# Expert weights by quarters of a head, w_query loaded once, and eight places for gathered rows instead of sixteen

## The chip, the cores and the metric

The kernel runs on one core of one Trainium2 chip, in float32. The metric is device time in microseconds, the median of several executions.

## The reference, cut to what matters

One layer of an encoder over 512 tokens of 1024 numbers: adaLN, a mixing sub-layer (8 heads of neighbourhood attention, 4 of differential attention, one output projection `w_out`), a LayerNorm, and then PEER retrieval, in which each token picks 16 of 16384 experts in each of 8 heads. The change is about PEER and what leads into it:

```python
qc = (xc @ w_query).reshape(PEER_CHUNK, PEER_HEADS, 2, PEER_DKEY // 2)
s_half = jnp.einsum('chpk,pnk->chpn', qc, sub_keys, preferred_element_type=jnp.float32)
top_s, top_i = lax.top_k(s_half, PEER_TOPK)
cand_s = (top_s[:, :, 0, :, None] + top_s[:, :, 1, None, :]).reshape(PEER_CHUNK, PEER_HEADS, -1)
cand_i = (top_i[:, :, 0, :, None] * PEER_NKEYS + top_i[:, :, 1, None, :]).reshape(PEER_CHUNK, PEER_HEADS, -1)
best_s, best_j = lax.top_k(cand_s, PEER_TOPK)
expert = jnp.take_along_axis(cand_i, best_j, axis=-1)
g = jax.nn.softmax(best_s, axis=-1)
u_e = expert_down[expert]
act = jax.nn.gelu(jnp.einsum('chkd,cd->chk', u_e, xc), approximate=False)
v_e = expert_up[expert]
return jnp.einsum('chk,chkd->cd', (g * act).astype(xc.dtype), v_e)
```

`w_query` is 1024 x 2048, `expert_down` and `expert_up` are 16384 x 1024. After PEER, `x = LN(alpha*x + (1+gate)*f)`, scaled by `ln2_g` and shifted by `ln2_b`.

## The kernel before, in words

Tokens lie in four tiles of 128, one token on each partition. A first phase (`FIRST_GROUPS`, made by `phase_a_groups`) does the modulation, the input projection, and attention as 48 items of a tile and a head (`ATT`). A group is a piece of PE work that ends in one PSUM bank and is evacuated by DVE (kinds in `ON_DVE`) or ACT. `FIRST_TILE` sets groups of tile 0's mixing output and its PEER query between the attention items: mix_t and out at items 17 and 18, the transposed u at 28, four query groups at 30 to 33, key scores at 34. `LN_FIRST` and `CHOOSE_FIRST` do the same for DVE: tile 0's LayerNorm at items 19 to 25, the choice of experts of head 0 at items 36 to 43.

A "head" from here on is one of 32 pairs of a tile and a PEER head, in the order of `HEAD_AT` (tile 0 heads 0 to 3, tile 1 heads 0 to 3, tile 0 heads 4 to 7, and so on). `choose(head, step)` (L1078) does top-k on DVE in 16 steps: it writes 16 expert numbers per token to `expert_idx`.

The second phase is a stream of 1024 gathers, 512 "down" and 512 "up" (16 a head). Each is one indirect DMA from POOL (L594) that fetches one expert row of 4 KB for each of 128 tokens, 0.524 MB, into a place. `gather_order` (L190) sets their order: down `at`, then up `at - UP_LAG`, with `UP_LAG` 19. POOL waits in `wait_for_place` (L572) until the place's last use is over. The first 280 gathers go round eight places (`FIRST_PLACES`); then eight more are added, in the slots of `w_out` (`OUT_SLOT`), which POOL does after a wait for out(3,1) (L591).

Who uses what:
- DVE runs the loop at L1323. For each down it makes the dot product with the token's u (L1334), which frees the place. In the first eight dots of a head it also chooses the next head, two steps a dot. `weigh` (L1285) stands after the third dot of the next head (`WEIGH_AT`) and makes that head's 16 weights at once. `LN_AT` and `ADD_AT` set tiles' LayerNorms and mixing adds after given dots, `RESIDUAL_AFTER` the residual (L1296) and, a head later, `finish` (L1313) of a tile.
- ACT waits for 16 dots and runs one gelu per head (`expert_gelu`, L852), the next head's exponentials (`gate`, L844), and 16 `diagonals` (L974): each is the identity scaled by one weight. It also evacuates PE's groups, `EVAC_AFTER` 3 diagonals behind the step in which the group ended, and takes the square roots (`ln_deviation`, `deviation`).
- PE runs the loop at L801. For each up it multiplies the diagonal by the gathered row, in two halves of 512 (L810; each is two matmuls in the profile), into the tile's sum. Behind it, it does the parts that `SCHEDULE` (L133) gives to that step: transposes, query parts (L642), out parts (L668), key scores (L676). An entry is (first step, parts per step, groups); a query or out group has eight parts.
- SP loads weights. `w_query` comes in four chunks of 2.10 MB, and `QUERY_SLOT` has only two slots for them: chunks 0 and 1 before the stream and again in it, chunks 2 and 3 twice in it, eight loads (L486, L500, L509 to L517).

Of the kernel before, what the change touches and what calls it, by code (L numbers as in the profile page):

```python
# [19 lines left out]
ALU = mybir.AluOpType  # L20
# [50 lines left out]
QUERY_SLOT = [1, 0, 1, 0]  # L71
FIRST_PLACES, PLACES = 8, 16
UP_LAG = TOPK + 3
WEIGH_AT = 2
# [16 lines left out]
def octet_runs(t):  # L91
# [5 lines left out]
FIRST_TILE = {17: [("mix_t", (0, 0)), ("mix_t", (0, 1)), ("out", (0, 0))], 18: [("out", (0, 1))],  # L97
              28: [("u_first", (0,)), ("u_first", (1,))],
              30: [("query", (0, 0, 0, 1))], 31: [("query", (0, 1, 0, 1))], 32: [("query", (0, 2, 0, 1))],
              33: [("query", (0, 3, 0, 1))], 34: [("key_scores", (0, 0))]}  # L100
LN_FIRST = {19: (0,), 20: (1,), 21: (2,), 22: (3,), 23: (4,), 24: (5,), 25: (6, 7)}
CHOOSE_FIRST = {36 + i: (2 * i, 2 * i + 1) for i in range(8)}


def phase_a_groups():
# [9 lines left out]
    for a in range(len(ATT) + 3):  # L115
# [4 lines left out]
        if a >= 3:  # L120
            g += [("values", (a - 3,))]
        g += FIRST_TILE.get(a, [])
    g += [("mix_t", (1, s)) for s in range(2)] + [("out", (1, s)) for s in range(2)]
# [9 lines left out]
SCHEDULE = [(0, 4, [("u_t", (1, s)) for s in range(2)]),  # L133
            (4, 3, [("query", (0, b, 1, 1)) for b in range(4)]), (19, 1, [("key_scores", (0, 1))]),
            (20, 3, [("query", (1, b, 1, 1)) for b in range(4)]), (35, 1, [("key_scores", (1, 1))]),
            (36, 2, [("query", (2, b, 0, 2)) for b in range(4)]),
            (55, 1, [("key_scores", (2, 0))]), (58, 1, [("key_scores", (2, 1))]),
            (59, 1, [("mix_t", (2, s)) for s in range(2)]), (64, 1, [("out", (2, s)) for s in range(2)]),
            (80, 2, [("query", (3, b, 0, 2)) for b in range(4)]), (99, 1, [("key_scores", (3, t)) for t in range(2)]),
            (101, 1, [("mix_t", (3, s)) for s in range(2)]), (106, 1, [("out", (3, s)) for s in range(2)]),  # L140
            (144, 1, [("u_t", (t, s)) for t in (2, 3) for s in range(2)]),
            (150, 1, [("query", (0, b, 2, 2)) for b in range(4)]), (185, 1, [("key_scores", (0, t)) for t in (2, 3)]),
            (190, 1, [("query", (1, b, 2, 2)) for b in range(4)]), (223, 1, [("key_scores", (1, t)) for t in (2, 3)]),
            (230, 1, [("query", (2, b, 2, 2)) for b in range(4)]),
            (264, 1, [("key_scores", (2, 2))]), (312, 1, [("key_scores", (2, 3))]),
            (316, 1, [("query", (3, b, 2, 2)) for b in range(4)]), (349, 1, [("key_scores", (3, t)) for t in (2, 3)])]
# [43 lines left out]
def gather_order():  # L190

    order = []
    for at in range(SETS + UP_LAG):
        order += [("down", at)] if at < SETS else []
        order += [("up", at - UP_LAG)] if at >= UP_LAG else []
    return order
# [40 lines left out]
def build(nc, x, c, w_ada, b_ada, w_in, w_out, na_rpb, t5_bias, lambda_q1, lambda_k1, lambda_q2,  # L237
# [3 lines left out]
    with ctx:  # L241
# [55 lines left out]
        for slot in (T5_SLOT,) + tuple(OUT_SLOT):  # L297
            places += [w_flat[slot][:, i * D:(i + 1) * D] for i in range(4)]
# [1124 lines left out]
```

## Time and profile before

| | us |
|---|---|
| median of 3 runs | 1805.6 |
| their range | 1800.57 to 1809.73 |
| the profiled execution | 1808.22 |
| its span | 1806.1 |
| PE busy | 1487.8 (82%) |
| DVE busy | 1137.8 (63%) |
| POOL busy | 1004.0 (56%) |
| ACT busy | 386.9 (21%) |

The span runs from the first to the last instruction; the execution's own time is 2.1 us more. Shares are of the span. DMA moved 612.29 MB in it, of which 536.94 MB on the gathers' queue, a mean of 339 GB/s; 607.97 MB were read from HBM. The mean granted TensorE clock was 0.968.

### The profile page before, as it was taken

The numbers are of one execution on the slowest core, as the hardware profiler recorded it, in microseconds if no ns is written. First come the engines' busy times: TensorE is split into PE (matmuls) and PEld (weight loads), VectorE is DVE, ScalarE is ACT, GpSimd is POOL, SyncE is SP. The second block draws the span as 40 slices with busy tenths as digits, with TensorE's granted clock in tenths as the row PEclk, the third lists the DMA queues.
The fourth block names the chain that finished last, engine by engine and source line by source line (L and its number), as shares of the span: only waits on it lengthen the run. The fifth ranks groups of instructions, "written<-read, shape, count | busy, mean of one in ns | idle before, by whom it ended". The sixth has DMA issues, their size and how long they took to land.

```text
span 1806.1 us, 14345 instructions
## 1 busy us (share of the span) xinstructions
PE 1487.8 (82%) x4112; PEld 689.3 (38%) x4112; DVE 1137.8 (63%) x2715; ACT 386.9 (21%) x983; POOL 1004.0 (56%) x1057
## 2 busy tenths in 40 slices
PE   5899988974889898887988979877799777777776
PEld 4444455642445344332433434322343222222222
DVE  5453056679567576878666766677666666666741
ACT  1111143422122212312112221221212111111220
POOL 2100000034667676677776767777777777777770
PEclk9799999896999999999999999999999999999998
DMA  9677320166999999999999999999999999999992
GB/s 311 240 261 212 116 70 12 13 230 211 405 406 409 394 409 407 362 409 410 409 408 408 409 408 409 409 409 410 409 409 409 409 409 409 409 408 410 406 410 94
DMA packets 194307, 612.29 MB, mean 339 GB/s; under 512 B 31263, under 2 KB 31671, under 8 KB 194071
## 3 DMA queue, kind: packets, MB, share of 16 engines
q0 software_dynamic: 147456, 536.94, 75.2%
q1 hardware_dynamic: 46423, 73.21, 12.1%
q10 hardware_dynamic: 352, 1.25, 0.2%
q8 instruction: 34, 0.56, 0.1%
q14 instruction: 42, 0.34, 0.1%
HBM read 607.97 MB, written 3.34 MB: 338 GB/s over the span
## 4 chain that ended last, share of the span: by engine, by line
DMA 40%; PE 26%; POOL 15%; DVE 8%; issue 7%; ACT 1%; SPq 1%; DVEq 0%; POOLq 0%
DMA big<-in_expert_up,expert_idx 14%; DMA region_v<-in_expert_up,expert_idx 13%; PE pair L604 11%; POOL big L594 10%; PE pair L810 10%; DMA big<-in_expert_down,expert_idx 8%; POOL region_v L594 4%; DMA region_v<-in_expert_down,expert_idx 4%; PE pair L642 2%; DVE big L1334 2%; DMA big<-in_w_ada 1%; PE pair L668 1%; DVE region_v L1334 1%; ACT big L907 1%; DVE big L1242 1%
## 5 line engine op out<-in xcount | busy, mean ns | idle before, releaser
L810 PE MATMUL pair<-big 128*128 128x512 f32 x1416 | 690.8, 612 | 181.4 <-DMA big<-in_expert_up,expert_idx 139.4
L1334 DVE CUSTOM_DVE_ANT_0 big<-big,pair 128x1024 f32<-128x1024 f32 x346 | 421.8, 1220 | 273.9 <-DMA big<-in_expert_down,expert_idx 272.5
L810 PEld LDWEIGHTS pair<-big 128*128 128x128 f32 x1416 | 244.7, 190 | 554.5 <-issue 485.1
L594 POOL DMA_INDIRECT big<-in_expert_up,expert_idx x354 | 336.4, 950 | 142.4 <-PE pair L810 83.8
L594 POOL DMA_INDIRECT big<-in_expert_down,expert_idx x346 | 330.6, 956 | 122.9 <-issue 99.4
L810 PE MATMUL pair<-region_v,big 128*128 128x512 f32 x632 | 308.6, 612 | 64.5 <-DMA region_v<-in_expert_up,expert_idx 63.3
L1334 DVE CUSTOM_DVE_ANT_0 region_v<-region_v,pair 128x1024 f32<-128x1024 f32 x166 | 202.5, 1220 | 130.9 <-DMA region_v<-in_expert_down,expert_idx 129.2
L604 PE MATMUL pair<-big 128*128 128x512 f32 (+1 forms) x496 | 203.9, 605 | 1.9 <-DVE big L1210 1.9
L594 POOL DMA_INDIRECT region_v<-in_expert_down,expert_idx x166 | 161.9, 975 | 69.6 <-issue 45.1
L981 ACT ACTIVATE big<-ident,big 128x128 f32<-128x128 f32 x512 | 158.5, 389 | 187.8 <-DVE big L1293 185.9
L810 PEld LDWEIGHTS pair<-region_v,big 128*128 128x128 f32 x632 | 110.7, 190 | 223.7 <-issue 214.4
L560 POOL TENSOR_SCALAR small<-small 128x4 f32<-128x4 f32 (+1 forms) x7 | 1.6, 233 | 348.2 <-DVE small L1266 289.9
L594 POOL DMA_INDIRECT region_v<-in_expert_up,expert_idx x158 | 149.9, 949 | 67.2 <-PE pair L810 35.4
L642 PE MATMUL pair<-big 128*128 128x256 f32 (+1 forms) x640 | 144.3, 342 | 6.9 <-DVE big L1058 6.1
L642 PEld LDWEIGHTS pair<-big 128*128 128x128 f32 x640 | 107.3, 195 | 96.1 <-issue 87.1
L604 PEld LDWEIGHTS pair<-big 128*128 128x128 f32 (+1 forms) x496 | 88.2, 198 | 100.3 <-issue 96.5
L890 ACT ACTIVATE big<-pair 128x512 f32<-128x512 f32 (+2 forms) x74 | 33.3, 456 | 415.8 <-PE pair L642 262.0
L855 ACT ACTIVATE big<-big 128x16 f32<-128x16 f32 x32 | 6.9, 216 | 456.1 <-DVE big L1334 456.0
L1179 DVE SCALAR_TENSOR_TENSOR big<-big,small 128x512 f32<-128x512 f32 x78 | 62.2, 798 | 2.8
L958 ACT ACTIVATE big<-pair 128x512 f32<-128x512 f32 (+3 forms) x70 | 37.6, 541 | 120.0 <-PE pair L604 99.7
L668 PE MATMUL pair<-big 128*128 128x512 f32 x128 | 60.8, 594 | 1.6 <-ACT big L890 1.6
L907 ACT ACTIVATE big<-big,small 128x256 f32<-128x256 f32 (+1 forms) x64 | 39.0, 610 | 73.8 <-DVE small L1242 73.8
(145 smaller groups left out, 1008.0 us busy)
## 6 DMA issues: line engine op xcount, KB each, us to landing
big<-in_w_ada SPq DMA_DIRECT2D x12, 2048.0 KB, 15.6
big<-in_w_query SPq DMA_DIRECT2D x8, 2048.0 KB, 19.1
big<-in_w_in SPq DMA_DIRECT2D x6, 2048.0 KB, 15.9
big<-in_expert_up,expert_idx POOLq DMA_INDIRECT x354, 17.7
big<-in_expert_down,expert_idx POOLq DMA_INDIRECT x346, 17.7
big<-in_w_out SPq DMA_DIRECT2D x2, 2048.0 KB, 10.3
big<-na_scr SPq DMA_DIRECT2D x24, 128.0 KB, 4.0
region_v<-in_expert_down,expert_idx POOLq DMA_INDIRECT x166, 12.9
```

Of the source, the lines that this page charges most:

```text
L594: nc.gpsimd.indirect_dma_start(places[place], None, (expert_down if kind == "down" else expert_up)[0], bass.IndirectOffsetOnAxis(expert_id ...
L604: last = nc.tensor.matmul(ps, a, b, start=(i == 0), stop=(i == len(pairs) - 1))
L642: return nc.tensor.matmul(ps[:, 0:n * P], w_slot[QUERY_SLOT[c]][:, k, b * P:(b + 1) * P], src, start=(k == 0), stop=(k == KB - 1))
L668: return nc.tensor.matmul(ps[:, :], src, w_slot[OUT_SLOT[s]][:, k, :], start=(k == 0), stop=(k == KB - 1))
L810: last = nc.tensor.matmul(pair[t % 2][:, s * HALF:(s + 1) * HALF], diag[:, j, :], places[place][:, s * HALF:(s + 1) * HALF], start=(h == 0 ...
L890: nc.scalar.activation(dst, ps, ACT.Copy).then_inc(act_evac, 1)
L907: nc.scalar.activation(exps, raw, ACT.Exp, bias=row_min[:, slot:slot + 1], scale=-1.0, accum_out=row_sum[:, slot:slot + 1]).then_inc(exp_d ...
L958: nc.scalar.activation(dst, ps, ACT.Copy, scale=scale).then_inc(act_evac, 1)
L981: nc.scalar.activation(diag[:, j, :], ident[:, :], ACT.Copy, scale=weights[:, head % 2, j:j + 1]).then_inc(diag_done, 1)
L1179: last = v.scalar_tensor_tensor(out=acc, in0=w[:, k, :], scalar=c_exp[:, k:k + 1], in1=acc, op0=ALU.mult, op1=ALU.add)
L1242: v.tensor_tensor_reduce(out=dst, in0=scored, in1=bias, scale=1.0, scalar=3.0e38, op0=ALU.add, op1=ALU.min, accum_out=row_min[:, slot:slot ...
L1334: v.tensor_tensor_reduce(out=places[place], in0=places[place], in1=u_cur[:, :], scale=1.0, scalar=0.0, op0=ALU.mult, op1=ALU.add, accum_ou ...
```

## The change

Nothing else of the result changes; these parts of the order and of the storage do:
- `QUERY_SLOT` gives each chunk of `w_query` a slot of its own; chunks 2 and 3 take the slots of `w_out` once out(3,0) and out(3,1) are done. There are four loads instead of eight.
- Eight places throughout, with no wait for out(3,1) on POOL.
- gelu, weighing and diagonals go by quarters of a head (four dots). The ups follow their downs by 7 instead of 19; the first up comes after down 14, then two ups for each down until they have caught up.
- Tile 0's LayerNorm, query and key scores stand one to five items earlier in attention; heads 0 and 1 are both chosen there (items 32 to 47). out(1,1) moves from ahead of PE's loop into its first steps; the other groups of `SCHEDULE` move, and so do LayerNorms, adds and residuals.
- In the LayerNorms of the second phase and tile 0's, (x - mean) * rstd * gain + shift is two operations on DVE instead of three.

```diff
-QUERY_SLOT = [1, 0, 1, 0]
-FIRST_PLACES, PLACES = 8, 16
-UP_LAG = TOPK + 3
-WEIGH_AT = 2
+QUERY_SLOT = [1, 0] + OUT_SLOT
+PLACES = 8
+QUARTER = 4
+UP_LAG = QUARTER + 3
+FIRST_UP = 14
...
+FIRST_TILE = {16: [("mix_t", (0, 0)), ("mix_t", (0, 1)), ("out", (0, 0))], 17: [("out", (0, 1))],
+              25: [("u_first", (0,)), ("u_first", (1,))],
+              26: [("query", (0, 0, 0, 1))], 27: [("query", (0, 1, 0, 1))], 28: [("query", (0, 2, 0, 1))],
+              29: [("query", (0, 3, 0, 1))], 30: [("key_scores", (0, 0))]}
+LN_FIRST = {18: (0,), 19: (1,), 20: (2, 3, 4), 21: (5,), 22: (6, 7)}
+CHOOSE_FIRST = {32 + i: (i // 8, 2 * (i % 8)) for i in range(16)}
...
+SCHEDULE = [(0, 1, [("out", (1, 1))]), (14, 1, [("mix_t", (2, s)) for s in range(2)]),
+            (22, 4, [("u_t", (1, s)) for s in range(2)]),
+            (24, 4, [("query", (0, b, 1, 1)) for b in range(4)]), (34, 1, [("key_scores", (0, 1))]),
+            (35, 4, [("query", (1, b, 1, 1)) for b in range(4)]), (45, 1, [("key_scores", (1, 1))]),
+            (46, 2, [("out", (2, s)) for s in range(2)]),
+            (56, 1, [("mix_t", (3, 0))]), (59, 1, [("mix_t", (3, 1))]), (62, 1, [("out", (3, s)) for s in range(2)]),
+            (80, 2, [("query", (2, b, 0, 2)) for b in range(4)]), (98, 1, [("key_scores", (2, t)) for t in range(2)]),
+            (100, 1, [("query", (3, b, 0, 2)) for b in range(4)]), (133, 1, [("key_scores", (3, t)) for t in range(2)]),
...
+LN_FROM = {1: 21, 2: 88, 3: 168}
+ADD_AT = {8: (1, 0), 20: (1, 1), 60: (2, 0), 65: (2, 1), 81: (3, 0), 89: (3, 1)}
+RESIDUAL_AFTER = {12: 0, 16: 1, 28: 2}
+WEIGHED = [max(QUARTER * (n + 1), 13) for n in range(HEADS * QUARTER - 1)]
...
+    for at in range(SETS):
+        order.append(("down", at))
+        for _ in range(2):
+            if at >= FIRST_UP and ups <= at - UP_LAG:
+                order.append(("up", ups))
+                ups += 1
+    order += [("up", at) for at in range(ups, SETS)]
...
-            load_query(2, ("query", (0, 3, 1, 1)))
-            load_query(3, ("query", (1, 3, 1, 1)))
-            load_query(0, ("query", (2, 3, 0, 2)))
-            load_query(1, ("query", (3, 3, 0, 2)))
+            load_query(2, ("out", (TILES - 1, 0)))
+            load_query(3, ("out", (TILES - 1, 1)))
...
-            load_query(2, ("query", (0, 3, 2, 2)))
-            load_query(3, ("query", (1, 3, 2, 2)))
...
-            def expert_gelu(head):
-                act.wait_ge(dot_done, (head + 1) * TOPK)
-                nc.scalar.activation(acts[:, head % 2, :], at_head(dots, head), ACT.Gelu).then_inc(gelu_done, 1)
+            def expert_gelu(head, q):
+                lo = q * QUARTER
+                act.wait_ge(dot_done, head * TOPK + lo + QUARTER)
+                nc.scalar.activation(acts[:, head % 2, lo:lo + QUARTER], at_head(dots, head)[:, lo:lo + QUARTER],
+                                     ACT.Gelu).then_inc(gelu_done, 1)
...
             for head in range(HEADS):
+                for q in range(QUARTER):
+                    if head * QUARTER + q in deviation_before:
+                        ln_deviation(deviation_before[head * QUARTER + q])
+                    expert_gelu(head, q)
+                    diagonals(head, q)
+                    if q == 2 and head + 1 < HEADS:
+                        gate(head + 1)
...
+            def weigh(head, q):
+                k, lo = head % 2, q * QUARTER
+                if q == 0:
+                    dve.wait_ge(gate_done, head + 1)
+                    link(v.reciprocal(gate_sum[:, k:k + 1], gate_sum[:, k:k + 1]))
+                    if head >= 2:
+                        dve.wait_ge(diag_done, (head - 1) * TOPK)
+                dve.wait_ge(gelu_done, head * QUARTER + q + 1)
+                v.scalar_tensor_tensor(out=weights[:, k, lo:lo + QUARTER], in0=gate_exps[:, k, lo:lo + QUARTER],
+                                       scalar=gate_sum[:, k:k + 1], in1=acts[:, k, lo:lo + QUARTER],
+                                       op0=ALU.mult, op1=ALU.mult).then_inc(weight_done, 1)
```

## Rows read from the trace of the kernel before

**Rows 1.** The page: DMA's busy tenths and GB/s in 40 slices.
```profile
DMA  9677320166999999999999999999999999999992
GB/s 311 240 261 212 116 70 12 13 230 211 405 406 409 394 409 407 362 409 410 409 408 408 409 408 409 409 409 410 409 409 409 409 409 409 409 408 410 406 410 94
```

**Rows 2.** The page: the chain that ended last, by engine.
```profile
DMA 40%; PE 26%; POOL 15%; DVE 8%; issue 7%; ACT 1%; SPq 1%; DVEq 0%; POOLq 0%
```

**Rows 3.** Windows: us, busy (count) by engine, PEclk, DMA share, GB/s.
```profile
384.50:450.00 65.50, 34.65 (x136) 21.45 (x135) 59.05 (x140) 12.05 (x29) 34.56 (x34) 0.77 0.77 259
450.00:600.00 150.00, 130.56 (x426) 70.15 (x424) 90.10 (x217) 30.03 (x82) 101.28 (x108) 0.98 1.03 405
600.00:625.00 25.00, 21.41 (x54) 9.91 (x55) 15.84 (x44) 11.42 (x27) 15.26 (x17) 0.86 1.01 383
625.00:725.00 100.00, 92.67 (x260) 47.02 (x258) 68.42 (x162) 15.79 (x42) 71.47 (x75) 1.00 1.03 409
725.00:750.00 25.00, 20.09 (x46) 8.00 (x47) 19.50 (x36) 7.52 (x16) 15.35 (x16) 1.00 0.88 324
800.00:1750.00 950.00, 768.80 (x1777) 303.24 (x1776) 651.90 (x1538) 192.14 (x500) 692.73 (x728) 1.00 1.03 409
```

**Rows 4.** DMA issues (450:600, 1200:1500, page): count, KB, us to landing.
```profile
region_v<-in_expert_down,expert_idx POOLq DMA_INDIRECT x28, 7.9
...
big<-in_expert_up,expert_idx POOLq DMA_INDIRECT x86, 18.1
...
big<-in_w_query SPq DMA_DIRECT2D x8, 2048.0 KB, 19.1
```

**Rows 5.** Groups of instructions by form: busy, mean ns, idle before.
```profile
L981 ACT ACTIVATE big<-ident,big 128x128 f32<-128x128 f32 x512 | 158.5, 389 | 187.8 <-DVE big L1293 185.9 <-PE pair L810 1.9
...
L855 ACT ACT_TABLE_LOAD x32 | 41.1, 1283 | 0.6
...
L1293 DVE SCALAR_TENSOR_TENSOR big<-big 128x16 f32<-128x16 f32 x32 | 7.5, 235 | 1.1
...
L855 ACT ACTIVATE big<-big 128x16 f32<-128x16 f32 x32 | 6.9, 216 | 456.1 <-DVE big L1334 456.0
```

**Rows 6.** Timeline, start of the stream: start, us, engine, line.
```profile
384.46 1.22 POOL L594 DMA_INDIRECT region_v<-in_expert_down,expert_idx  x1 [0.20 <-issue]
...
389.16 1.22 DVE L1334 CUSTOM_DVE_ANT_0 region_v<-region_v,pair 128x1024 f32<-128x1024 f32 x1 [2.13 <-DMA region_v<-in_expert_down,expert_idx]
...
407.32 0.68 DVE L1058 TENSOR_TENSOR big<-pair,mods 128x512 f32<-128x512 f32 x1
...
438.83 3.75 PE L810 MATMUL pair<-big 128*128 128x512 f32 x4 [23.47 <-ACT big L981]
```

**Rows 7.** Timeline of PE: three query parts; an up, an out part.
```profile
466.41 0.83 PE L642 MATMUL pair<-big 128*128 128x128 f32 x6
...
628.80 1.88 PE L810 MATMUL pair<-region_v,big 128*128 128x512 f32 x4
630.52 1.02 PE L668 MATMUL pair<-big 128*128 128x512 f32 x2
```

**Rows 8.** Timeline at the dip: DVE waits for ACT.
```profile
731.63 0.16 DVE L1039 RECIPROCAL small<-small 128x1 f32<-128x1 f32 x1 [4.01 <-ACT small L842]
```

**Rows 9.** Windows of attention, tiles 2 and 3, by the first scores of each.
```profile
303.80:343.40 39.60, 34.59 (x225) 28.11 (x224) 23.96 (x79) 17.83 (x52) 2.08 (x4) 0.91 0.20 27
343.40:379.60 36.20, 28.81 (x143) 18.91 (x142) 29.74 (x115) 17.06 (x51) 1.28 (x2) 0.86 0.04 18
```

**Rows 10.** The tail: timeline, a piece of the chain, a window.
```profile
1755.32 1.22 DVE L1334 CUSTOM_DVE_ANT_0 big<-big,pair 128x1024 f32<-128x1024 f32 x1 [1.32 <-DMA big<-in_expert_down,expert_idx]
...
1756.71 34.59 PE pair L810 x80
...
1795.99 0.81 DVE L1317 TENSOR_SCALAR big<-big,small 128x1024 f32<-128x1024 f32 x1
...
1770.00:1781.00 11.00, 11.00 (x27) 4.93 (x26) 0.00 (x0) 0.00 (x0) 0.00 (x0) 1.00 0.07 29
```

More of the change, by code:

```diff
@@ L122, in phase_a_groups @@
         g += FIRST_TILE.get(a, [])
-    g += [("mix_t", (1, s)) for s in range(2)] + [("out", (1, s)) for s in range(2)]
+    g += [("mix_t", (1, s)) for s in range(2)] + [("out", (1, 0))]
     g += [("u_t", (0, s)) for s in range(2)]
@@ L132 @@
 FIRST_GROUPS = phase_a_groups()
[L133 to L146, printed above, removed]
@@ L190, in gather_order @@
 def gather_order():
[L192 to L195, printed above, removed]
+    order, ups = [], 0
+    for at in range(SETS):
[5 more added lines that the diff above has]
+    order += [("up", at) for at in range(ups, SETS)]
     return order
 GATHERS = gather_order()
-FIRST_GATHERS = 280
 PLACE_OF, LAST_USE, USES = {}, {}, {}
@@ L296, in build @@
         places = [region_v[:, i, :] for i in range(4)]
-        for slot in (T5_SLOT,) + tuple(OUT_SLOT):
-            places += [w_flat[slot][:, i * D:(i + 1) * D] for i in range(4)]
+        places += [w_flat[T5_SLOT][:, i * D:(i + 1) * D] for i in range(4)]
         na_place_sb = mods[0:T5_BUCKETS, 0:2, :].rearrange("p t (e m) -> p (t e) m", m=2 * P)
@@ L628, in query_weights @@
             def query_weights(c, first, n):
-                loads = {(0, 0): 1, (0, 1): 1, (1, 0): 1, (1, 1): 1, (2, 0): 2, (3, 0): 2, (0, 2): 3, (1, 2): 3,
-                         (2, 2): 4, (3, 2): 4}[c, first]
+                loads = 1 if c < 2 else 2
                 slot = QUERY_SLOT[c]
@@ L893, in _ @@
                 ps = bank_of(g)
+                if (kind, args) == ("mix_t", (1, 1)):
+                    gate(0)
                 if kind in ("u_first", "mix_t", "u_t", "query", "key_scores"):
@@ L972, in _, with diagonals @@
                       .then_inc(t5_written, 16)
-            def diagonals(head):
-                act.wait_ge(weight_done, head + 1)
-                for j in range(TOPK):
+            def diagonals(head, q):
+                act.wait_ge(weight_done, head * QUARTER + q + 1)
+                for j in range(q * QUARTER, (q + 1) * QUARTER):
                     at = head * TOPK + j
@@ L1280, in _ @@
                         ln_step(0, step)
[L1281 to L1294 removed]
+                    if args[0] in CHOOSE_FIRST:
+                        head, step = CHOOSE_FIRST[args[0]]
+                        choose(head, step)
+                        choose(head, step + 1)
+            def weigh(head, q):
[9 more added lines that the diff above has]
+                                       op0=ALU.mult, op1=ALU.mult).then_inc(weight_done, 1)
             def residual(t):
@@ L1336, in _ @@
                                            accum_out=dots[:, at:at + 1]).then_inc(dot_done, 1)
-                    if j == WEIGH_AT and head > 0:
-                        weigh(head - 1)
-                    if j < TOPK // 2 and head + 1 < HEADS:
+                    for n in range(WEIGHED.count(at)):
+                        first = WEIGHED.index(at) + n
+                        weigh(first // QUARTER, first % QUARTER)
+                    if 0 < head < HEADS - 1 and j < TOPK // 2:
                         choose(head + 1, 2 * j)
                         choose(head + 1, 2 * j + 1)
-                    for group in ADD_AT.get(at, ()):
-                        add_mix(*group)
-                    if j >= TOPK // 2 and head in LN_AT:
-                        ln_step(LN_AT[head], j - TOPK // 2)
+                    if at in ADD_AT:
+                        add_mix(*ADD_AT[at])
+                    for row_tile, first in LN_FROM.items():
+                        if 0 <= at - first < 8:
+                            ln_step(row_tile, at - first)
                 if head in RESIDUAL_AFTER:
```

74 lines of the change are left out of this document (25 added, 49 removed).

## The prediction

> **What bounds the kernel now.** I read the page's slices first. From slice 20 of 40 on, DMA stands at 9 tenths and some 409 GB/s in every slice but the last [rows 1]. The chain that ended last says the same: 40% is DMA, 15% POOL, which issues the gathers, 26% PE [rows 2]. In 950 us late in the stream PE is busy 769 and DVE 652 [rows 3]. So from about 385 us on the kernel is a stream of 1024 gathers of 0.524 MB, and at 409 GB/s each costs 1.28 us, a down and an up together 2.56. The windows then show where the stream is not full: 259 GB/s in the first 65.5 us, 383 and 324 GB/s in two stretches of 25 us, 405 between [rows 3]. Against 409 that is 24.0, 1.6, 5.2 and 1.5 us, 32 us lost. Behind the stream, from 1781 to 1806, is a tail of 25 us in which PE, and then DVE, work alone. Ahead of it attention is bound by the chain PE, DVE, ACT, not by DMA.
>
> **Loads of w_query: eight become four.** Each moves 2.10 MB [rows 4]; two of the four that stay are loaded before the stream or at its start, as now. Four fewer run beside a full DMA: 4 x 2.10 MB / 409 GB/s = 20.5 us off the path, -20.5. The median of 19.1 us to landing is shared time and not the price. The first kept load (chunk 2) is issued after step 69 and needed at step 80: 11 x 2.56 = 28 us against those 19 us, covered by 9 us; if that cover went, PE would wait. The load of chunk 3 has over 20 steps. SP then goes to the ln2 rows at the 176th dot, needed at the 208th, 82 us later.
> The Trainium skill, DMA: Bandwidth & Descriptors, section Specifications, gives a core about 358 GB/s from HBM; by it the four loads would be worth an estimated 23.4 us. The trace moves 409 GB/s for 950 us on end, so the measurement decides.
>
> **Eight places instead of sixteen.** Up to the 280th gather the kernel already runs on eight: issue to landing is then 7.9 us, later 18.1 [rows 4], and between 625 and 725 us eight places gave the same 409 GB/s as sixteen do [rows 3]. In steady state I cost this at nothing. What shrinks is tolerance. A gather issued into an idle DMA is used 4.7 us after its issue [rows 6], 3.4 without its own 1.28. A place comes round after 8 x 1.28 = 10.3 us, so a consumer must be done 10.3 - 1.28 - 3.4 = 5.6 us after landing: DVE (1.22 for a dot) may be 4.4 us late, PE (1.9 for an up) 3.7. Later than that, DMA idles one for one.
> The Trainium skill, same page, Anatomy of one DMA - SWDGE (gpsimd) path, gives 2.0 us plus the bytes for a transfer, an estimated 3.2 us where the row shows 4.7. By it each stall below would be 1.5 us shorter, the sum some 6 us lower; the row decides.
>
> **Work by quarters.** There are 96 more gelus (0.22 us, ACT) and 96 more weighings (0.23 us, DVE) [rows 5]. Table loads stay at two a head, since gate comes once a head between two gelus. DVE is busy 652 of 950 us [rows 3], so idle for 31% of a quarter's 10.3 us, 3.2 us, and holds a weighing of 0.23 us with a link of the same order. A quarter's gelu is issued at its last dot and needed one dot later, 2.56 us; ACT's quarter is 0.22 + 4 x 0.39 us. Where ACT evacuates a PE group it waits for that step's up, which lands seven downs behind; most groups end one step before a multiple of four, which leaves two downs of room. Cost 0 in steady state.
>
> **The start of the stream.** Now head 1 is chosen between its first eight dots: from the first dot (389.16) to the mixing add (407.32) are 18.2 us, 8 dots take 9.2, so one choice is 9.0 us of DVE. Adds and LayerNorm of tile 1 follow, and the first up stands at 438.83 [rows 6]. After the change downs 0 to 13 need only their dots (1.2 against 1.28 us), and up 0 lands near 408. Ups then come two for each down, one per 1.92 us, while PE does the eight parts of out(1,1): 1.72 (628.80 to 630.52) + 0.86 for an out part's two matmuls, 2.57 us a step [rows 7]. It falls 5 us behind and up to 9 with the wait for its start: about 4 us beyond the tolerance. The three weighings after dot 13 pass through ACT's diagonals in turn, about 3.5 us of DVE: 2 lost. PE starts after idling; the first up at 438.83, after 23 us idle, took 3.75 us instead of 1.9: 3 us. With the fill of 3.4 us that makes 12.4 instead of 24.0. Bounds: 3.4 and 24.
> Later, the parts of queries 0 and 1 of tile 1 go four to a step: three took 0.83 us [rows 7], four make 1.72 + 1.11 = 2.83, in eight steps 2.2 us late, within tolerance. out(2,.) goes two parts a step: 1.72 + 1.72 = 3.43 us, eight times 0.87 = 7 us late; 3.3 beyond, with a rest from before it 4.5 lost. The dip at 732 is DVE waiting 4 us for ACT's deviation, behind ACT's evacuations [rows 8]; LayerNorm 2 (dots 88 to 95) still meets query groups, LayerNorm 3 no longer does. With three residuals (4 us of DVE each) I take 4 us, bounds 0 and 12. Together 8.5 where the trace has 8.3. Losses go from 32.3 to 20.9: -11.4.
>
> **Attention.** Two choices lie there instead of one. Tile 3 gets 12 pairs of steps instead of 8, tile 2 four instead of none, each 9.0/8 = 1.1 us: 4.5 us each. DVE is busy 30 of 36 us in tile 3, 24 of 40 in tile 2 [rows 9], so I take 4 and 0.5: +4.5, bounds 9.0 (nothing hidden) and -2 (the fused LayerNorm alone: two operations of 0.8 us, as in [rows 10], and out(1,1) gone from ahead of the loop).
>
> **The tail.** The last dot starts at 1755.32, and PE then runs 80 matmuls, 20 ups, in 34.6 us, 0.43 each, from 1756.71 to 1791.3 [rows 10]. Those 20 gathers need 25.6 us from 1755.2, to 1780.8, so PE ends 10.5 us after the last landing. (In the window from 1770 to 1781 only 29 GB/s are left, about one sixteenth of 409: 15 of 16 DMA engines are done, and I take it that the last one sets the landings, before and after.) With seven ups behind the last down, PE has eight from 1.3 us after its landing: 1.5 + 8 x 1.72 = 15.3 us, against 8 x 1.28 = 10.3: 5.0 after the last landing. The last quarter's diagonals are ready by 3 us. -5.4. In finish one 0.81 us operation goes: -0.8. Bounds: 0 and -9.
>
> **Sum:** -20.5 - 11.4 + 4.5 - 5.4 - 0.8 = -33.6. The profiled execution took 1808.2 us (span 1806.1), so 1774.6 of its kind; the median of the three runs, 1805.6, lies 2.6 lower: 1772.
>
> **Rivals.**
> (a) The start goes smoothly: PE and DVE keep up, only the fill is lost, and attention hides both choices. Losses of 10 instead of 21 and 4.5 less in attention give 1757, at the extreme 1750. For it: DVE's first dots have nothing beside them. Against: PE's own 2.57 us a step.
> (b) The start gives nothing back: the same 24 us go on weighings, PE's slow start and out(2,.), and attention pays all 9.0. 1772 + 11.4 + 4.5 = 1788, with later stalls up to 1795. For it: DVE in tile 3 is at 82%, and the tolerance is exceeded in three places.
> (c) No change: (b), and each of 32 heads stalls 0.5 us because gate, two table loads (2.6 us) and gelu do not fit before the weighing: 1804.
> (d) Slower: the ring of eight starves by quarters. DVE stands at gelu_done, dots stop, places are not freed. It decides once a quarter costs DMA over 33.6/127 = 0.26 us; at 0.5 us it is 64 us, 1836. Against it: 409 GB/s on eight places, and 3.2 us of DVE idle per quarter. For it: those had 16 diagonals ready ahead, and in the half of a head with choosing DVE needs 1.2 + 1.1 of 2.56 us.
> That the loads are only moved can be excluded: the diff has four issues.
>
> **How the numbers follow.** Forecast (1761 to 1783) 0.52, (a) 0.16, (b) 0.20, (c) 0.06, (d) 0.06. A measurement of this kernel can tell about 0.5%, 9 us, from no change. The range takes the forecast with (a) and (b): 1750 to 1795. All three are faster by over 0.5%: 0.88; (c) 0.06; (d) 0.06.
>
> **What would show it.** Four issues of w_query; the stretch from 600 us on at 409 GB/s with 7 to 8 us to landing; the first up before 415 us; over 300 GB/s in the first 65 us; dips while out(2,.) runs; 32 matmuls after the last dot and PE's end some 15 us after it; tile 3 of attention near 40 us. Wrong: issue to landing under 7 us or below 405 GB/s late in the stream (d), DVE idle before its weighing above 0.5 us per quarter (c, d), a first gather after 394 us (b).

## The result, and the profile after

The changed kernel takes 1785.0 us (median of four executions, 1782.4 to 1785.1), the one before in the same comparison 1807.7 (four, 1800.6 to 1810.1). The ratio is 0.9873, with a 95% interval of 0.9856 to 0.989: 22.6 us less, where the forecast had 33.6. It lies in the range (1750 to 1795), between the forecast and rival (b). The profiled execution took 1785.1, its span 1782.6.

From the page of the changed kernel: DMA's slices, the chain by engine, the gelu of the quarters, and two DMA issues with their us to landing.

```profile
DMA  9668310139999999999999999999999999999995
GB/s 307 250 248 227 122 71 1 25 121 356 387 396 356 385 375 387 409 409 409 408 391 407 410 409 378 407 410 409 409 408 409 378 409 409 409 409 400 409 409 218
...
DMA 37%; PE 31%; POOL 15%; issue 8%; DVE 5%; ACT 1%; SPq 1%; DVEq 0%; POOLq 0%
...
L848 ACT ACTIVATE big<-big 128x4 f32<-128x4 f32 x128 | 26.1, 204 | 501.5 <-DVE big L1338 501.4
...
big<-in_w_query SPq DMA_DIRECT2D x4, 2048.0 KB, 15.3
...
region_v<-in_expert_down,expert_idx POOLq DMA_INDIRECT x256, 7.9
```

Against [rows 1, 2, 4] this is still a stream bound by DMA, with four loads instead of eight and 7.9 us to landing throughout. The tenth to the sixteenth slice, 356 to 396 GB/s, are where it is not full for long; later only single slices fall, to 378 at the lowest. Its windows (from:to us, then length, busy time and count of PE, PEld, DVE, ACT and POOL, granted clock, DMA share, GB/s):

```profile
384.50:450.00 65.50, 54.16 (x189) 32.02 (x190) 39.13 (x89) 15.44 (x40) 39.12 (x42) 0.90 0.92 336
450.00:600.00 150.00, 135.40 (x430) 66.64 (x429) 106.79 (x254) 40.59 (x101) 104.79 (x110) 1.00 0.99 379
600.00:625.00 25.00, 21.19 (x49) 8.44 (x48) 14.49 (x37) 5.84 (x14) 15.90 (x17) 1.00 1.03 404
625.00:725.00 100.00, 86.34 (x242) 42.38 (x241) 69.84 (x168) 25.94 (x65) 64.68 (x68) 1.00 0.99 384
725.00:750.00 25.00, 23.34 (x60) 10.38 (x59) 15.64 (x33) 6.47 (x17) 18.41 (x20) 1.00 1.03 409
800.00:1750.00 950.00, 773.53 (x1790) 305.39 (x1791) 664.23 (x1622) 223.49 (x585) 686.40 (x727) 1.00 1.02 405
1755.00:1760.00 5.00, 5.00 (x13) 2.28 (x12) 0.00 (x0) 2.50 (x5) 1.11 (x2) 1.00 1.02 405
1760.00:1765.00 5.00, 5.00 (x13) 2.15 (x12) 0.00 (x0) 0.00 (x0) 0.00 (x0) 1.00 0.11 45
```

Beside [rows 3]: the start has risen from 259 to 336 GB/s, although the first gather now goes out at 392.0 us and no longer at 384.5. The dip at 732 is gone (409 for 324). In its place 450 to 600 us have fallen from 405 to 379, and 625 to 725 from 409 to 384. Late in the stream there are 405 for 409. The first up, which the forecast had near 408 us, and a window around it:

```profile
419.29 3.40 PE L802 MATMUL pair<-big 128*128 128x512 f32 x4 [3.19 <-ACT big L977]
...
419.00:423.00 4.00, 3.71 (x6) 1.71 (x7) 1.53 (x5) 3.42 (x14) 0.34 (x1) 0.60 1.04 411
```

The tail, from the timeline (start, us, engine, line, operation; in brackets how long the engine was idle before it and until what):

```profile
1753.18 1.22 DVE L1338 CUSTOM_DVE_ANT_0 big<-big,pair 128x1024 f32<-128x1024 f32 x1 [1.33 <-DMA big<-in_expert_down,expert_idx]
...
1754.56 7.11 PE L802 MATMUL pair<-region_v,big 128*128 128x512 f32 x16 [0.60 <-DMA region_v<-in_expert_up,expert_idx]
...
1761.51 7.03 PE L802 MATMUL pair<-big 128*128 128x512 f32 x16
...
1768.57 1.29 DVE L1306 TENSOR_TENSOR big<-pair,mods 128x512 f32<-128x512 f32 x2 [13.67 <-PE pair L802]
...
1773.24 1.28 DVE L1320 SCALAR_TENSOR_TENSOR big<-big,small,mods 128x1024 f32<-128x1024 f32 x1
1774.56 1.28 DVE L1324 SCALAR_TENSOR_TENSOR big<-big,small,mods 128x1024 f32<-128x1024 f32 x1
1775.88 4.92 SPq L516 DMA_DIRECT2D out_x<-big  x8
```

After the last dot stand 32 matmuls and not 80, and PE ends at 1768.54, 15.4 us after that dot's start; before it was 36.0 [rows 10].

**Where the 23.5 us between the two spans went**, taking the last landing as the last dot's start and the ups behind it at 1.28 us each (20 before, 8 now: 1780.8 and 1763.4; the trace has the last gather landed at 1780.6 and 1763.3): ahead of the first gather +7.5; from there to the last landing 1396.3 became 1371.4, -24.9; from there to PE's end 10.5 became 5.1, -5.4; finish, up to the store, 8.0 became 7.3, -0.7. The store behind it takes 6.7 in both.

**Where the stream loses**: the time from the first gather's issue to the 1024th, beyond 1.282 us for each, by stretches of gathers, worked out from the issue times on POOL. With sixteen places the issues run ahead of the landings, so the order of before stands here with eight (experiment 1). What loads of w_query take at 5.1 us each is already left out: four and two in the second and third stretch of before, two and none after. The last column is the last version of experiment 9.

| gathers | before, eight places | after | experiment 9 |
|---|---|---|---|
| 0 to 63 | 24.2 | 8.3 | 5.9 |
| 64 to 255 | 4.5 | 15.5 | 3.0 |
| 256 to 543 | 7.7 | 11.1 | 10.1 |
| 544 to 1023 | 12.5 | 6.9 | 5.9 |
| sum | 48.9 | 41.8 | 24.9 |

The start gives back 16 us, and 14 are lost again between gathers 64 and 543. The sums differ by 7.1 and the last landings, less the loads, by 4.4: in experiment 1 the last gathers are issued at PE's pace, 1.72 us apart, and the last of them lands 5.1 us after its issue, in the changed kernel 7.8.

### The profile page after: what moved, and what is told of

The parts are those of the page before. It is cut to its first block, busy times and chain, and to the rows that moved or that the text cites. A ratio compares the mean times of both kernels' runs of the same rounds, so it can differ in the third digit from the quotient of the medians.

```text
span 1782.6 us, 14587 instructions
## 1 busy us (share of the span) xinstructions
PE 1490.9 (84%) x4112; PEld 686.2 (38%) x4112; DVE 1143.0 (64%) x2799; ACT 428.8 (24%) x1089; POOL 994.6 (56%) x1057
## 4 chain that ended last, share of the span: by engine, by line
DMA 37%; PE 31%; POOL 15%; issue 8%; DVE 5%; ACT 1%; SPq 1%; DVEq 0%; POOLq 0%
DMA region_v<-in_expert_up,expert_idx 20%; PE pair L802 13%; DMA big<-in_expert_up,expert_idx 13%; PE pair L597 12%; POOL big L587 8%; POOL region_v L587 7%; PE pair L660 2%; DMA region_v<-in_expert_down,expert_idx 2%; DMA big<-in_expert_down,expert_idx 2%; PE pair L634 1%; DMA big<-in_w_ada 1%; DVE region_v L1338 1%; PE pair L751 1%; PE pair L740 1%; SPq L446 1%
## 5 line engine op out<-in xcount | busy, mean ns | idle before, releaser
L802 PE MATMUL pair<-big 128*128 128x512 f32 x1024 | 499.5, 611 | 111.2 <-DMA big<-in_expert_up,expert_idx 105.0
L802 PE MATMUL pair<-region_v,big 128*128 128x512 f32 x1024 | 496.6, 608 | 106.3 <-DMA region_v<-in_expert_up,expert_idx 102.8
L1338 DVE CUSTOM_DVE_ANT_0 big<-big,pair 128x1024 f32<-128x1024 f32 x256 | 312.3, 1220 | 211.5 <-DMA big<-in_expert_down,expert_idx 209.2
L1338 DVE CUSTOM_DVE_ANT_0 region_v<-region_v,pair 128x1024 f32<-128x1024 f32 x256 | 311.9, 1219 | 152.4 <-DMA region_v<-in_expert_down,expert_idx 147.7
L802 PEld LDWEIGHTS pair<-big 128*128 128x128 f32 x1024 | 176.4, 190 | 378.0 <-issue 328.1
L802 PEld LDWEIGHTS pair<-region_v,big 128*128 128x128 f32 x1024 | 175.2, 189 | 374.4 <-issue 365.3
L587 POOL DMA_INDIRECT big<-in_expert_up,expert_idx x256 | 246.0, 961 | 109.0 <-PE pair L802 71.1
L587 POOL DMA_INDIRECT region_v<-in_expert_up,expert_idx x256 | 240.3, 939 | 100.4 <-PE pair L802 68.0
L587 POOL DMA_INDIRECT region_v<-in_expert_down,expert_idx x256 | 240.9, 941 | 97.7 <-issue 73.1
L587 POOL DMA_INDIRECT big<-in_expert_down,expert_idx x256 | 242.0, 945 | 88.3 <-issue 74.3
L634 PEld LDWEIGHTS pair<-big 128*128 128x128 f32 x640 | 106.2, 194 | 99.6 <-issue 92.9
L660 PE MATMUL pair<-big 128*128 128x512 f32 x128 | 63.0, 612 | 1.8 <-ACT big L884 1.0
## 6 DMA issues: line engine op xcount, KB each, us to landing
big<-in_w_query SPq DMA_DIRECT2D x4, 2048.0 KB, 15.3
```

Of the source, the lines that this page charges most:

```text
L587: nc.gpsimd.indirect_dma_start(places[place], None, (expert_down if kind == "down" else expert_up)[0], bass.IndirectOffsetOnAxis(expert_id ...
L634: return nc.tensor.matmul(ps[:, 0:n * P], w_slot[QUERY_SLOT[c]][:, k, b * P:(b + 1) * P], src, start=(k == 0), stop=(k == KB - 1))
L660: return nc.tensor.matmul(ps[:, :], src, w_slot[OUT_SLOT[s]][:, k, :], start=(k == 0), stop=(k == KB - 1))
L802: last = nc.tensor.matmul(pair[t % 2][:, s * HALF:(s + 1) * HALF], diag[:, j, :], places[place][:, s * HALF:(s + 1) * HALF], start=(h == 0 ...
L1338: v.tensor_tensor_reduce(out=places[place], in0=places[place], in1=u_cur[:, :], scale=1.0, scalar=0.0, op0=ALU.mult, op1=ALU.add, accum_ou ...
```

## The experiments

Medians stand against the kernel before on the same chip (1806.5 to 1806.9 us there) and, as a difference, against the changed kernel's 1785.0. Between them lie a few us of noise: half a per cent is 9 us, and the start of the stream alone varies by up to 6 us from execution to execution (last section). Where it matters, the trace's own account is given beside the median: the time from the first gather's issue to PE's end, 1376.5 us in the changed kernel. In the edits, "..." stands for lines left out.

**1. Before, with eight places throughout.** Is the smaller ring a cost?

```diff
-FIRST_PLACES, PLACES = 8, 16
+FIRST_PLACES, PLACES = 8, 8
-                if n == FIRST_GATHERS:
-                    pool.wait_ge(pe_group, INDEX[("out", (TILES - 1, 1))] + 1)
```

> The kernel before, but with eight places for the whole stream. Theory (in steady state eight places carry the same 409 GB/s; sixteen only absorb lateness): the late stalls of the kernel before now reach DMA, some 5 us in all, and the eight gathers of place 150 are no longer waited for, so 1805 to 1815 us, with issue to landing near 7.9 us throughout. Rival (the eight places cost by themselves at every quarter or head, 0.5 us or more for each of the heads 9 to 31): 1820 us or above, with windows below 405 GB/s where no LayerNorm, residual or key scores stand.

Measured: 1806.1 (ten executions), ratio 0.9993 (0.9979 to 1.0008). Eight places cost nothing, as the sum had it. From its page, where before had 18.1 us [rows 4]:

```profile
region_v<-in_expert_down,expert_idx POOLq DMA_INDIRECT x258, 7.9
```

The eight further places only made each gather wait longer in the queues. Late in the stream the two do differ: from 800 to 1750 us this version moves 406 GB/s where before moved 409 [rows 3]. That rate buys before nothing: it falls to 29 GB/s at the end, while the last gathers land [rows 10]. From the first gather's issue to the last dot the traces have 1370.9 us with sixteen places and 1368.4 with eight, to the last landing 1396.1 and 1395.9.

**2. After, with the four loads back.** Chunks 0 to 3 are loaded a second time, though the data is there.

```diff
+            load_query(0, ("query", (0, 3, 1, 1)))
+            load_query(1, ("query", (1, 3, 1, 1)))
...
+            load_query(2, ("query", (2, 3, 0, 2)))
+            load_query(3, ("query", (3, 3, 0, 2)))
...
-                loads = 1 if c < 2 else 2
+                loads = (1 if c < 2 else 2) + first // 2
```

> The changed kernel with four more loads of w_query of 2.10 MB each, chunks 0 and 1 loaded again after their use for tile 1, chunks 2 and 3 after their use for tiles 0 and 1, and waited for where they are used next. Theory (DMA bound, a load costs its bytes): 4 x 2.10 MB / 409 GB/s = 20.5 us more than the changed kernel's 1785, that is 1803 to 1808. Rival (loads run in time that the stream loses anyway, by stalls of eight places): 5 to 12 us more, 1790 to 1797.

Measured: 1803.9 (ten), ratio 0.9995 (0.9978 to 1.0011): +18.8, 4.7 a load. Its profiled execution, one of the slowest (1809.3), has 25.5 us more from the first gather to PE's end, so some stalls come with the loads there.

**3. Before, with four of its eight loads left out.** The same cost from the other side.

```diff
-            load_query(0, ("query", (2, 3, 0, 2)))
-            load_query(1, ("query", (3, 3, 0, 2)))
...
-            load_query(2, ("query", (0, 3, 2, 2)))
-            load_query(3, ("query", (1, 3, 2, 2)))
...
```

> The kernel before with four of its eight loads of w_query left out: chunks 0 and 1 are not loaded again after chunks 2 and 3, nor those again for tiles 2 and 3, so the queries of tiles 2 and 3 and of half of tile 0 and 1 use the wrong chunk. Everything else, waits and order, is as before. Theory (DMA bound): 20.5 us less than 1806.5, that is 1785 to 1788, the whole of what the change gained. Rival (sixteen places and the late bound of one DMA engine hide part of it): 1790 to 1797.

Measured: 1785.3 (1780.1 to 1787.0), ratio 0.9879 (0.9853 to 0.9906), so -21.7, 5.4 a load; from the first gather to PE's end its trace has 22.8 us less than before's. With wrong chunks other expert rows are fetched, as many and as large. With experiment 2 this brackets 4 x 5.1 = 20.5. It also lands on the changed kernel's time: the four loads are worth the whole gain, and all else that the change does comes to nothing together.

**4. After, with out(2,.) one part a step** (and what stands behind it in the schedule, and DVE's adds of these parts, some steps later).

```diff
-            (46, 2, [("out", (2, s)) for s in range(2)]),
-            (56, 1, [("mix_t", (3, 0))]), (59, 1, [("mix_t", (3, 1))]), (62, 1, [("out", (3, s)) for s in range(2)]),
-            (80, 2, [("query", (2, b, 0, 2)) for b in range(4)]), (98, 1, [("key_scores", (2, t)) for t in range(2)]),
+            (46, 1, [("out", (2, s)) for s in range(2)]),
+            (62, 1, [("mix_t", (3, 0))]), (65, 1, [("mix_t", (3, 1))]), (68, 1, [("out", (3, s)) for s in range(2)]),
+            (84, 2, [("query", (2, b, 0, 2)) for b in range(4)]), (100, 1, [("key_scores", (2, t)) for t in range(2)]),
...
-ADD_AT = {8: (1, 0), 20: (1, 1), 60: (2, 0), 65: (2, 1), 81: (3, 0), 89: (3, 1)}
+ADD_AT = {8: (1, 0), 20: (1, 1), 62: (2, 0), 72: (2, 1), 87: (3, 0), 94: (3, 1)}
```

> The changed kernel with tile 2's output projection at one part a step (steps 46 to 61) instead of two (46 to 53), and what follows it moved back: mix_t of tile 3 to steps 62 and 65, its output projection to 68 to 83, query chunk 2 to 84 to 99, chunk 3 to 102 to 129. Tile 2's LayerNorm stays where it is. Theory (two parts take PE 3.43 us a step against 2.56 of the stream, and mix_t behind them holds ACT, then DVE 6.1 us at dot 64): the stretch at 525 to 600 us comes back to 405 GB/s, 6 to 9 us are gained, 1776 to 1779. Rival (DVE at dots 56 to 72, with a choice, two adds and the copy of u, is what is late): no more than 2 us gained.

Measured: 1776.0 (1771.8 to 1776.6), ratio 0.9828 (0.9801 to 0.9855): -9.1. First the changed kernel's timeline at the stall that this removes (the first row: ACT idle 12.59 us until PE's transposed mix), with two rows of its windows:

```profile
569.87 0.60 ACT L884 ACTIVATE big<-pair 128x512 f32<-128x512 f32 x1 [12.59 <-PE pair L650]
570.49 1.28 ACT L841 ACT_TABLE_LOAD   x1
...
572.11 1.28 ACT L848 ACT_TABLE_LOAD   x1
...
573.40 0.20 ACT L848 ACTIVATE big<-big 128x4 f32<-128x4 f32 x1
573.64 0.24 DVE L1295 SCALAR_TENSOR_TENSOR big<-big 128x4 f32<-128x4 f32 x1 [6.09 <-ACT big L848]
...
525.00:600.00 75.00, 67.67 (x178) 30.25 (x177) 52.80 (x134) 16.89 (x47) 48.26 (x52) 1.00 0.96 357
```

And the window of experiment 4:

```profile
525.00:600.00 75.00, 69.79 (x183) 31.09 (x182) 55.69 (x140) 19.99 (x54) 54.32 (x58) 1.00 1.00 395
```

The chain runs PE, ACT, DVE, POOL, DMA. PE does 1.88 us for the up and as much for two parts of out, and falls behind step by step. ACT takes its work in a fixed order, and the evacuation of mix_t(3,0) stands in it ahead of the next gate and gelu; it waits until PE gets there. DVE stands 6.09 us at its weighing, no dot is made, no place comes free. A queue of 7.9 us bridges part of that; 357 GB/s is the rest. In this version no wait of DVE before a weighing is longer than 4.3 us, and from the first gather to PE's end the trace has 7.7 us less. The edit moves the adds too, so it does not by itself separate PE from them (the rival of its expectation); what speaks for PE is the first row above, in which ACT waits 12.59 us for PE.

**5. After, with tile 2's LayerNorm at dots 72 to 79** instead of 88 to 95, ahead of the query groups.

```diff
-LN_FROM = {1: 21, 2: 88, 3: 168}
+LN_FROM = {1: 21, 2: 72, 3: 168}
```

> The changed kernel with tile 2's LayerNorm at dots 72 to 79 instead of 88 to 95, where ACT has no group of PE to evacuate between its diagonals. Theory (the 335 GB/s stretch around 650 us is DVE waiting for ACT's square root, which stands behind an evacuation that waits for PE): the waits of 6.1 and 3.4 us at the reciprocal go, and the kernel is 5 to 8 us faster than 1785: 1777 to 1780. Rival (the stretch is the two loads of w_query and PE's query parts, and DVE's wait is only their shadow): within 2 us of 1785.

Measured: 1778.6 (1774.5 to 1780.1), ratio 0.9843 (0.9815 to 0.987): -6.5. From the first gather to PE's end the trace has 4.7 us less, all of it between gathers 64 and 255. The changed kernel's timeline at this place: ACT has waited 10.80 us for a query group before it comes to the square root, DVE 6.09 us for that, and POOL 5.02 for DVE's dot.

```profile
653.07 0.38 ACT L884 ACTIVATE big<-pair 128x256 f32<-128x256 f32 x1 [10.80 <-PE pair L634]
...
655.05 0.29 ACT L834 ACTIVATE small<-small 128x1 f32<-128x1 f32 x1
...
655.38 0.16 DVE L1036 RECIPROCAL small<-small 128x1 f32<-128x1 f32 x1 [6.09 <-ACT small L834]
...
658.39 1.74 POOL L587 DMA_INDIRECT big<-in_expert_down,expert_idx  x1 [5.02 <-DVE big L1338]
```

All such waits of DVE together, in the changed kernel and then in experiment 5 (idle us, times):

```profile
  ACT small L834: 10.4, 3
```

```profile
  ACT small L834: 0.8, 1
```

**6. After, with out(1,1) ahead of PE's loop again**, where before had it.

```diff
-    g += [("mix_t", (1, s)) for s in range(2)] + [("out", (1, 0))]
+    g += [("mix_t", (1, s)) for s in range(2)] + [("out", (1, s)) for s in range(2)]
...
-SCHEDULE = [(0, 1, [("out", (1, 1))]), (14, 1, [("mix_t", (2, s)) for s in range(2)]),
+SCHEDULE = [(14, 1, [("mix_t", (2, s)) for s in range(2)]),
...
-ADD_AT = {8: (1, 0), 20: (1, 1), 60: (2, 0), 65: (2, 1), 81: (3, 0), 89: (3, 1)}
+ADD_AT = {8: (1, 0), 10: (1, 1), 60: (2, 0), 65: (2, 1), 81: (3, 0), 89: (3, 1)}
```

> The changed kernel with out(1,1) ahead of PE's loop as before, and not in its first eight steps. Theory (PE's 2.57 us a step with ups arriving one per 1.92 us is what makes downs 17 to 21 come every 5 us): the stretch from 425 to 450 us rises from 316 towards 390 GB/s, but the query of chunk 1 ends 7 us later, and 2 to 4 us are gained, 1781 to 1783. Rival (the weighings at dot 13 and ACT's diagonals bind there): the same 1785 within 1.5 us.

Measured: 1779.8 (1778.8 to 1782.9), ratio 0.9862 (0.9839 to 0.9884): -5.2, a little more than either expectation. In the changed kernel 425 to 450 us moved 316 GB/s with PE never idle; in this one:

```profile
425.00:450.00 25.00, 23.16 (x55) 9.44 (x54) 14.84 (x45) 2.85 (x9) 18.89 (x20) 1.00 0.98 382
```

PE's first steps of 2.57 us, while ups come two for each down, cost about 4 us in this stretch. Over the first 64 gathers the gain is 2.5 us (5.8 lost for 8.3), and to PE's end it is still 2.6. The rest of the median's 5.2 is not seen in the stream: this execution's first gather went out at 388.4 us instead of 392.0, which is within the scatter of the last section.

**7. After, with head 1 chosen between its first eight dots**, as before the change.

```diff
-CHOOSE_FIRST = {32 + i: (i // 8, 2 * (i % 8)) for i in range(16)}
+CHOOSE_FIRST = {36 + i: (0, 2 * i) for i in range(8)}
...
-                    if 0 < head < HEADS - 1 and j < TOPK // 2:
+                    if head < HEADS - 1 and j < TOPK // 2:
```

> The changed kernel with head 1 chosen between the first eight dots of the stream, as in the kernel before, and head 0 at items 36 to 43 of attention. Theory (the second choice costs attention 5 to 8 us and saves the start 9 us of DVE): the first gather starts at 385 to 388 us instead of 392, the first dots come every 2.3 us instead of 1.2, and the end is 2 to 6 us later than 1785, 1787 to 1791. Rival (the start is bound by PE's ups with out(1,1), so the choice beside the first dots is hidden): 3 to 6 us faster, 1779 to 1782.

Measured: 1783.4 (1783.0 to 1787.9), ratio 0.9883 (0.9859 to 0.9907): -1.7. Both expectations missed. The first gather went out at 382.4 us instead of 392.0, and the first 64 gathers lost 15.5 instead of 8.3 us. One choice costs DVE the same at either place, so moving it bought nothing.

**8. After, with the lag back at 19 for the last head**, so that 20 ups stand behind the last down.

```diff
-            if at >= FIRST_UP and ups <= at - UP_LAG:
+            if at >= FIRST_UP and ups <= at - (UP_LAG if at < SETS - TOPK else TOPK + 3):
```

> The changed kernel with the old lag at its end only: in the last head the ups wait until they are 19 behind, so 20 of them, instead of 8, stand behind the last down, as in the kernel before. The bytes and the gathers are the same. Theory (behind the last down PE needs 1.72 us for an up that arrives every 1.28): PE ends 80 matmuls or 34 us after the last dot instead of 15.4, the last dot comes 12 x 1.28 = 15.4 us earlier, and the time is 12 x 0.44 = 5.3 us more, 1789 to 1792. Rival (the last landing is set by one late DMA engine in either order): 1785 within 1.5 us.

Measured: 1787.7 (1786.3 to 1793.1), ratio 0.9906 (0.988 to 0.9933): +2.7, between the two expectations. Its timeline shows one more cost that the edit brings: while the lag grows, no ups come, PE is idle, and its granted clock falls to 0.50, the lower level of 1.2 GHz, so the first up afterwards takes 3.75 us and not 1.9.

```profile
1715.00:1728.00 13.00, 0.00 (x0) 0.00 (x0) 12.62 (x24) 3.17 (x11) 9.80 (x11) 0.61 1.03 410
1728.00:1733.00 5.00, 4.05 (x5) 1.85 (x6) 2.50 (x6) 0.66 (x2) 1.90 (x3) 0.50 1.03 409
1751.00:1763.00 12.00, 12.00 (x30) 5.30 (x29) 0.00 (x0) 0.00 (x0) 4.66 (x5) 1.00 0.82 299
...
1728.95 3.75 PE L802 MATMUL pair<-big 128*128 128x512 f32 x4 [15.96 <-DMA big<-in_expert_up,expert_idx]
...
1735.23 1.22 DVE L1338 CUSTOM_DVE_ANT_0 region_v<-region_v,pair 128x1024 f32<-128x1024 f32 x1 [1.31 <-DMA region_v<-in_expert_down,expert_idx]
...
1771.68 1.29 DVE L1306 TENSOR_TENSOR big<-pair,mods 128x512 f32<-128x512 f32 x2 [33.58 <-PE pair L802]
```

PE ends 36.4 us after the last dot, in the changed kernel 15.4: 21.0 more, for 12 x 1.28 = 15.4 us of gathers moved behind that dot, so 5.7 by the forecast's way of counting. The last landing does not come 25.6 us after the dot here, at 1760.8, but at 1763.3: with eight places the last gathers go out as PE frees places, 1.72 us apart, and DMA moves 299 GB/s beside a PE that is never idle (the third row). PE alone sets this tail. From the first gather's issue to PE's end the trace has 1384.1 us for 1376.5, 7.6 more; the median has only 2.7, and in the profiled execution the first gather went out 4.5 us earlier (387.5). The sign of the tail's term is thus shown by both, and its size by the traces alone.

**9. Three repairs, then four.** The first version has experiments 4 and 5, and moves the groups that ACT evacuates off steps that are multiples of four, such as:

```diff
-            (284, 1, [("key_scores", (2, 2))]), (324, 1, [("key_scores", (2, 3))]),
+            (285, 1, [("key_scores", (2, 2))]), (325, 1, [("key_scores", (2, 3))]),
```

> The changed kernel with both schedule edits (tile 2's LayerNorm at dots 72 to 79, output projections at one part a step) and the groups that ACT evacuates moved by one step, so that none ends in a step divisible by four (key scores at 101, 133, 213, 249, 285, 325, 361, transposed u at 173). Theory (each stall is DVE's weighing or LayerNorm behind an evacuation that waits for PE's step): the gains add, 6.5 + 9.1, and the two stretches near 1090 and 1390 us lose their 4 us waits, 3 to 5 us more: 1764 to 1768. Rival (the stream has one slack that both edits share): 1771 to 1775, no better than the better edit alone.

Measured: 1769.3 (1765.2 to 1774.5), ratio 0.9807 (0.978 to 0.9835): -15.7, where experiments 4 and 5 alone add to 15.6. It lies between the two expectations: the further 3 to 5 us for the move off the multiples of four are not seen in the median. The trace shows what the move does. DVE's waits before its weighings are 11.1 us in 8 where the changed kernel has 29.5 in 14, the two of 4 us near 1094 and 1386 us are gone, and from gather 256 on the stream loses some 2 us less. With experiment 6 too:

> The three edits that gained, together: tile 2's LayerNorm at dots 72 to 79, output projections at one part a step with no evacuated group in a step divisible by four, and out(1,1) ahead of PE's loop. Theory (separate stalls at separate places of the stream): 1769.3 less the 5.2 us of out(1,1), 1762 to 1766. Rival (the stream's start is bound by POOL and the fill once PE keeps up, so that out(1,1) gives nothing more): 1768 to 1770.

Measured: **1764.3** (1763.7 to 1768.2), ratio 0.9774 (0.9754 to 0.9795). It beats the changed kernel by 20.7 us (16.8 from the first gather to PE's end) and the kernel before by 2.3%. Its GB/s line, to be laid beside the first one above:

```profile
GB/s 308 256 242 224 138 72 1 25 112 358 402 396 400 403 404 410 409 409 409 403 409 395 410 409 409 387 410 409 409 409 409 401 408 409 402 407 394 411 409 217
```

**10. The same, with head 1 chosen in the stream** (the edit of experiment 7).

> The kernel a_best11 with head 1 chosen between the first eight dots of the stream instead of in attention. Theory (the 9 us of a choice cost as much in one place as in the other, since DVE is at 82% or more in both): within 3 us of a_best11. Rival (with PE's out(1,1) gone from the loop, DVE's first dots now set the start): 4 to 8 us slower than a_best11.

Measured: 1765.8 (1765.3 to 1770.4), ratio 0.9783 (0.9763 to 0.9804): the same within 2 us, as in experiment 7.

## Why the prediction was right, and where it was not

- **Bound by DMA, loads priced by their bytes: right.** -20.5 was put down; removing them from before gave -21.7, putting them back +18.8 (in single traces -22.8 and +25.5). It is the only large term, and it alone makes up the gain.
- **Eight places cost nothing: right**, by experiment 1, though not because eight move the same 409 GB/s all along: they move 406, and the kernel with sixteen loses as much at its end.
- **Quarters cost nothing in steady state: mostly right.** Rival (c) needed a stall of 0.5 us in every head, rival (d) over 0.26 us in every quarter. DVE stands before its weighing for 29.5 us in all, in 14 of 128 quarters, which is 0.23 a quarter, and 18.8 of it in four waits of over 4 us. Late in the stream the changed kernel moves 405 GB/s where before had 409: 1% of 950 us, 9 us. The same stretch with eight places and whole heads moved 406, so the quarters are at most a small part of it.
- **The start: too cautious.** 12.4 us of losses were put for 24.0; the first 64 gathers now lose 8.3 where they lost 24.2. The slow step was found where the forecast had it, PE with out(1,1), "about 4": experiment 6 gave 2.5 in the stream and 5.2 in the median. The first up came at 419.3 us, later than the forecast's 408 and its sign of 415; it was slow (3.40 us, at a granted clock of 0.60 from 419 to 423), but DMA was still full then (411 to 413 GB/s from 410 to 423), so its 3 us did not show.
- **The later stalls: the term that failed.** "Together 8.5 where the trace has 8.3" was the sentence. Between gathers 64 and 543 the table has 26.6 us for 12.2. Two costs were mis-sized. For out(2,.) PE's own lateness was counted, 7 us less the tolerance, 4.5; experiment 4 gave 9.1 in the median and 7.7 in its trace. For LayerNorms and residuals 4 us were taken; tile 2's LayerNorm alone was 6.5 in experiment 5's median and 4.7 in its trace. Both times the sum followed the late engine and not the one that waits for it in order: ACT stood at an evacuation, 12.59 and 10.80 us, with a gelu or a square root behind it for which DVE was waiting. The forecast had read exactly this pattern at 732 us [rows 8] and let it go with the groups that moved, without asking where the new schedule makes it anew. Start and later stalls together came to -4.4 (-24.9 less the loads' -20.5), not -11.4.
- **Attention: +7.5 for +4.5**, within the bounds of -2 and 9. Experiment 7 shows that the choice gained nothing by moving: 9.6 us earlier in attention, 7.2 more in the stream. Without the second choice its first gather is 2.0 us ahead of before's, the forecast's lower bound, and with it 9.6 us later, where the forecast had half hidden. Six executions with this attention code average 390.2 us, 5.7 later than before. How much of the 7.5 is the change and how much one execution's scatter stays open.
- **The tail: right.** 15.3 us from the last dot to PE's end were forecast, 15.4 are there, and its price of PE behind the last dot, 5.4, was 5.7 when experiment 8 put it back. Its parenthesis, that one late DMA engine sets the landings before and after, holds at most before (last section); and finish was -0.7 for -0.8.

So the sum missed by 11 us: about 7 in the stream, 3 in attention; the rest is how profiled execution and median lie to each other. Rival (b) had the attention and the stalls nearer; its start that gives nothing back was wrong by 16 us.

## What to carry to other kernels

In a stream that DMA bounds, price a transfer by its bytes at the stream's rate, wherever it is issued and however long it takes to land; here everything else in a large rewrite together came to nothing. A ring of places needs to cover the latency: here eight, 10.3 us of transfers, did as well as sixteen at 7.9 us to landing (fewer were not tried). When work on in-order engines is rescheduled, list for each evacuation what stands behind it on its engine and who waits for that, and place heavy steps so that none of these waits meets a step for which the other engine is late: the edits of schedule numbers in experiment 9 were worth 20.7 us in the medians and 17 in the traces, nearly as much as the four loads.

## What was not expected of the hardware

- **With sixteen places the sixteen DMA engines do not end together.** In the kernel before, the last 10 us of gathers moved one sixteenth of the rate [rows 10]. Experiment 3, the other version with sixteen places, does the same, 16 to 24 us after its last dot (first row below). Experiment 1, with eight, moves 294 GB/s until its last landing (second row), and the changed kernel falls from 405 to 45 to 0 within 10 us. So in these traces the stretch at one sixteenth comes with the longer ring, in two of two profiled executions; with eight places such a stretch lasts 3 us at most before the last landing, in all eleven. That one engine falls behind and a longer ring lets the others run ahead of it would fit, but it is not shown. PE, which is busy all that time, ends 36.0 us after the last dot with either ring.

```profile
1749.00:1757.00 8.00, 8.00 (x20) 3.50 (x19) 0.00 (x0) 0.00 (x0) 0.00 (x0) 1.00 0.07 27
1770.00:1780.00 10.00, 10.00 (x25) 4.45 (x24) 0.00 (x0) 0.00 (x0) 3.64 (x4) 1.00 0.82 294
```

- **The start of the stream scatters.** With attention's code unchanged from the changed kernel's, the first gather went out between 386.4 us (experiment 9, first version) and 392.3 (experiment 5), and the three executions with before's code lay at 384.2 to 384.8. A difference of 2 or 3 us between two kernels here is not to be read as an effect, and one of up to 6 in the first gather's issue neither.
- **A reordering can bring the slow clock back in the middle of a full stream.** In experiment 8 PE is idle for 16 us near the end and comes back at a granted clock of 0.50: 0.94 us a matmul for four of them, not 0.43 to 0.49. The forecast had counted this only for the start of the stream [rows 6].
